# A decoder trunk on one Trainium2 core: PE's expert sum three groups behind its dots in place of two, U gathers six experts ahead of V gathers in place of four

## The chip, the cores and the metric

The kernel runs as one launch on one core of a Trainium2 chip. The metric is the device time of the launch in microseconds (us); lower is better. Everything is float32.

## What is computed

Two layers of a decoder trunk on 512 prompt tokens and 32 sample tokens (8 sequences of 4), model width 1024. Each layer is a modulated RMSNorm, one input projection that feeds a gated delta recurrence and a sliding-window attention, an output projection, and then a retrieval of experts, which is the part that the change touches:

```python
def _peer(h, wq, sub_keys, u_tab, v_tab):
...
    q = (xf @ wq).reshape(T, PK_HEADS, 2, PK_HALF).astype(f32)
    s = jnp.einsum('thpd,hpnd->thpn', q, sub_keys.astype(f32))
...
    eidx = jnp.take_along_axis(cidx, pos, axis=-1).reshape(T, PK_HEADS * PK_TOPK)
    gate = jax.nn.softmax(top_s, axis=-1).reshape(T, PK_HEADS * PK_TOPK)
...
    def block(args):
        xt, it, gt = args
        a = jnp.einsum('td,tkd->tk', xt.astype(f32), u_tab[it].astype(f32))
        a = jax.nn.gelu(a, approximate=False) * gt
        return jnp.einsum('tk,tkd->td', a, v_tab[it].astype(f32))
```

Every token picks 128 experts. For each of them a row of 1024 numbers is gathered from table U and dotted with the token's vector; the gelu of the dot times a gate is the weight with which a row gathered from table V is added to the token's sum.

## The kernel before, in words

**Units.** The tokens are worked through in ten units (`DUES`): per layer four tiles of 128 prompt tokens and one tile of the sample tokens. A unit's trunk (everything but the expert stage) is cut by names that all engines share, the seams: `norm1`, `conv0` to `conv2`, `hswq`, `hz`, `hmisc` for the head of the next unit, then `swq`, `z`, `misc`, `qkv`, `qk`, `decay`, `kk`, `half0`/`level0` to `half6`/`level6`, `ks`, `rhs`, `state`, `scores`, `softmax`, `pv`, `wo`, `norm2`, `wq0` to `wq3`, `keys`. The head of unit u+1 is interleaved with the end of the top-k of unit u (`tail`, on DVE: `pairs`, `halves`).

**Rounds.** The experts of a unit are worked in groups of G = 2. A prompt unit has 64 groups, a sample unit 16, 544 in all. Group i belongs to an earlier unit than the trunk that runs beside it. `due(u)` (line 93) deals the groups out over the seams: each engine's program calls its own `step(i)` at the same seam, 54 steps to a trunk unit of layer one, 48 to the first of layer two and 64 to the others. Nothing but semaphores ties the engines; the order on each is fixed by the program.

**One step.** DVE (line 1124): multiplies the gelu of group i-1 with its gates (`gated`, line 1088, row L1092), then dots group i (row L1133, two of them). ACT (line 728): makes the diagonal matrices of group i-1 (`diagonals`, row L725, two of them), then waits for the dots of group i and applies the gelu (row L733). PE (line 1391): adds group i-LAG into the two accumulator banks `ACC` (`add`, line 1378, row L1387, four matmuls per expert, since a float32 matmul of 512 columns shows as two rows for each of the two banks; eight per group). Pool (lines 500 to 536): sends the U gathers, and behind each the V gather of an earlier expert (rows L526, L535), 512 KB each.

```python
            for e in range(len(ROUNDS) * G + AHEAD_U):
...
                        pool.wait_ge(dots, i + 1)
...
                if e >= AHEAD_U:
                    v = e - AHEAD_U
...
                    pool.wait_ge(v_acc, v + 1)
```

**Rings.** All buffers of a group have R = 4 places: `ubuf`, `vbuf`, the weights `a4` and the diagonals `diag`. So the U gather of group i waits for the dots of group i-4, the V gather of an expert for the sum of the expert eight before it, and ACT's diagonals of group d (line 723, `act.wait_ge(v_acc, (i + 1) * G)`; the semaphore starts at 8) for PE's sum of group d-4.

**The end of a unit's experts.** DVE's `finish` (line 1108, rows L1115 and L1118) reads `ACC` once PE has added the unit's last group, and lets PE start the next unit's sum (`acc_free`, line 1383). It stands behind the dots of step k == 2 of the next unit's groups. ACT's `store` (row L714) writes the result at k == 4, and Pool loads the next unit's `xp` and `g2p` into the same buffers at k == LOAD_AT = 10 (rows L520, L521), after that store has landed. In the sample unit of each layer the indices, gates and token vectors make a trip through DRAM (`bounce` on SP), for which Pool and DVE wait ahead of the first group of that unit.

Of the kernel before, what the change touches and what calls it, by code (L numbers as in the profile page):

```python
# [40 lines left out]
G = 2  # L41
R = 4
SLOTS_UV = R * G
AHEAD_U = 4
LOAD_AT = 10
DUES = L * UNITS
LAG = 2
PG = EXPERTS // G
SG = PG // 4
LG = TILES * PG + SG  # L50
# [54 lines left out]
def trunk(nc, ins, outs):  # L105
    with ExitStack() as ctx:
# [185 lines left out]
        def closing(step, final):  # L292

            for i in range(DUE[-1], len(ROUNDS)):
                step(i)
                if i - DUE[-1] in (3, 5, 7):
                    final((i - DUE[-1] - 3) // 2)

        def place(u):
            return *divmod(u, UNITS), u % UNITS == TILES  # L300
# [165 lines left out]
        def _(pool):  # L466
# [32 lines left out]

            for e in range(len(ROUNDS) * G + AHEAD_U):  # L500
                if e < len(ROUNDS) * G:
# [4 lines left out]
                    if e % G == 0:  # L506
# [8 lines left out]
                        if k == LOAD_AT:  # L515
# [11 lines left out]
                                         in_offset=off).then_inc(u_in[e % SLOTS_UV], 16)  # L527
                if e >= AHEAD_U:
                    v = e - AHEAD_U
                    u, k = ROUNDS[v // G]  # L530
# [9 lines left out]
        def _(act):  # L540
# [167 lines left out]
            def store(u):  # L708

                layer, tile, batch = place(u)  # L710
                waiter(act, u)("x_out", 1)
                act.sem_inc(settled, 1)
                dst = outs["y"][tile] if u >= DUES - 2 else outs["xbuf"][layer + 1, tile]
                act.dma_start(dst, xp[:]).then_inc(s["x_stored"], 16)  # L714

            def final(n):
                act.wait_ge(fin_sq, n + 1)
                A.activation(ss, ss, ACT.Sqrt).then_inc(fin_root, 1)

            def diagonals(i):  # L720
                pick = sel if place(ROUNDS[i][0])[2] else ident
                act.wait_ge(ag_sb, i + 1)
                act.wait_ge(v_acc, (i + 1) * G)
                for j in range(G):
                    last = A.activation(diag[:, i % R, j, :], pick[:], ACT.Copy, scale=a4[:, i % R, 2, j:j + 1])  # L725
                last.then_inc(diag_sb, 1)

            def step(i):
                u, k = ROUNDS[i]
                if i:  # L730
                    diagonals(i - 1)
                act.wait_ge(dots, i + 1 + R)
                A.activation(a4[:, i % R, 1, :], a4[:, i % R, 0, :], ACT.Gelu).then_inc(gelu_sb, 1)  # L733
                if k == 2 and u == DUES - 1:
                    final(TILES - 1)
                if k == 4 and u:
                    store(u - 1)

            def modulation(l):
# [30 lines left out]
            act.wait_ge(const_in, 32)  # L770
            act.wait_ge(sel_in, 16)
            program(head, body, tail, step, modulation)
            closing(step, final)
            diagonals(len(ROUNDS) - 1)
            final(TILES)
# [4 lines left out]
        def _(dve):  # L780
# [307 lines left out]
            def gated(i):  # L1088

                u, k = ROUNDS[i]  # L1090
                dve.wait_ge(gelu_sb, i + 1)
                V.tensor_tensor(a4[:, i % R, 2, :], a4[:, i % R, 1, :], gates[:, u % 2, G * k:G * k + G],  # L1092
                                ALU.mult).then_inc(ag_sb, 1)
# [14 lines left out]
            def finish(u):  # L1108

                wait = waiter(dve, u)  # L1110
                groups = sum(1 for owner, k in ROUNDS if owner <= u)
                dve.wait_ge(v_acc, SLOTS_UV + G * groups)
                wait("xp_in", 32)
                for i in range(2):
                    last = V.tensor_tensor(g2p[:, 512 * i:512 * i + 512], ACC[i][:], g2p[:, 512 * i:512 * i + 512], ALU.mult)  # L1115
                last.then_inc(acc_free, 1)
                dve.wait_ge(acc_free, u + 1)
                last = V.tensor_tensor(xp[:], xp[:], g2p[:], ALU.add)  # L1118
                if u >= DUES - 2:
                    link(last)  # L1120
                    last = rms(TILES - 1 + u - (DUES - 2), xp[:])
                last.then_inc(s["x_out"], 1)

            def step(i):
                u, k = ROUNDS[i]
                if k == 0 and place(u)[2]:
                    dve.wait_ge(bounce_in, 16 * 12 * (u // UNITS + 1))
                if i:
                    gated(i - 1)
                for j in range(G):  # L1130
                    dve.wait_ge(u_in[i % R * G + j], (i // R + 1) * 16)
                    row = ubuf[:, i % R, j, :]
                    last = V.tensor_tensor_reduce(row, row, h2s[u], 1.0, 0.0, ALU.mult, ALU.add, a4[:, i % R, 0, j:j + 1])  # L1133
                last.then_inc(dots, 1)
                if k == 2 and u:
                    finish(u - 1)

            dve.wait_ge(const_in, 32)
            program(head, body, tail, step, modulation)
            closing(step, final)  # L1140
            gated(len(ROUNDS) - 1)
            finish(DUES - 1)
# [3 lines left out]
        def _(pe):  # L1146
# [231 lines left out]
            def add(i):  # L1378
                u, k = ROUNDS[i]
                end = SG if place(u)[2] else PG  # L1380
                pe.wait_ge(diag_sb, i + 1)
                if k == 0 and u:
                    pe.wait_ge(acc_free, u)
                for j in range(G):
                    pe.wait_ge(v_in[i % R * G + j], (i // R + 1) * 16)
                    for c in range(2):
                        last = T.matmul(ACC[c][:], diag[:, i % R, j, :], vbuf[:, i % R, j, 512 * c:512 * c + 512],  # L1387
                                        start=k + j == 0, stop=k == end - 1 and j == G - 1, skip_group_check=True)
                    last.then_inc(v_acc, 1)

            def step(i):
                if i >= LAG:
                    add(i - LAG)

# [3 lines left out]
            closing(step, lambda n: None)  # L1398
            for i in range(len(ROUNDS) - LAG, len(ROUNDS)):
                add(i)  # L1400
# [117 lines left out]
```

## Time and profile before

| | us |
|---|---|
| median of 3 runs | 4345.22 |
| lowest, highest | 4344.15, 4350.73 |
| the profiled execution, its own time | 4338.44 |
| its span, first to last instruction | 4336.6 |
| busy: PE | 3660.1 (84%) |
| busy: DVE | 2698.8 (62%) |
| busy: POOL | 2348.3 (54%) |
| busy: ACT | 1034.7 (24%) |
| mean granted TensorE clock | 0.932 of full |
| DMA, mean over the span | 352 GB/s |

Busy is the time in which an engine executed; register, branch and semaphore instructions are not in it. PE's clock is given as the share of full speed that was granted in a stretch. In a row of the timeline, the number in brackets is how long the engine had been idle just before, and behind the arrow stands what ended that idle time. A matmul row with x8 is one group of two experts.

### The profile page before, as it was taken

The page shows a single profiled execution, that of the slowest core. Times are in us where ns is not written, and L with a number is a line of the kernel's source. Part 1 is how long each engine was busy: PE and PEld are TensorE (multiplying, and loading weights), DVE is VectorE, ACT ScalarE, POOL GpSimd, SP SyncE. Part 2 cuts the span into 40 slices and gives each one's busy share as a digit, 9 for nine tenths or more (in the row PEclk, how much of TensorE's full clock was granted, in tenths as well). Part 3 has the DMA queues.
Part 4 walks back from the last instruction along what each step waited for, and adds up shares of the span by engine and source line. Part 5 has one row for each costly group of instructions (what it writes and reads, how often), then busy time and mean ns, then how long its engine had stood idle before and what let it go on. Part 6 is the DMA issues. An engine that isn't in the chain of part 4 may idle for free.

```text
span 4336.6 us, 45555 instructions
## 1 busy us (share of the span) xinstructions
PE 3660.1 (84%) x15180; PEld 2168.1 (50%) x15180; DVE 2698.8 (62%) x6307; ACT 1034.7 (24%) x2478; POOL 2348.3 (54%) x2218
## 2 busy tenths in 40 slices
PE   7778789888888888879888888888888888899766
PEld 1546356544644555656456444644564455456522
DVE  1234674876776586538667666776587657664575
ACT  0111322232132222112321322132213121312122
POOL 0000475477467547434764577467647764674455
PEclk9888899999999999889999999999999998998989
DMA  7626799999999999699999999999999999997988
GB/s 272 256 100 224 285 389 406 376 375 399 395 363 384 379 382 347 250 322 377 378 356 384 348 394 391 414 375 405 393 414 381 387 389 366 377 364 298 331 327 341
DMA packets 362538, 1527.72 MB, mean 352 GB/s; under 512 B 44952, under 2 KB 46872, under 8 KB 340512
## 3 DMA queue, kind: packets, MB, share of 16 engines
q0 software_dynamic: 316480, 1151.48, 69.7%
q1 hardware_dynamic: 39632, 316.42, 18.6%
q10 hardware_dynamic: 6192, 56.91, 3.5%
q8 instruction: 121, 1.98, 0.2%
q14 instruction: 113, 0.93, 0.1%
HBM read 1505.45 MB, written 21.22 MB: 352 GB/s over the span
## 4 chain that ended last, share of the span: by engine, by line
PE 48%; DVE 21%; DMA 14%; issue 7%; POOL 6%; ACT 4%; SPq 0%; DVEq 0%; POOLq 0%; ACTq 0%
PE ACC L1387 20%; DVE ubuf L1133 6%; PE B L1191 6%; DMA vbuf<-in_peer_v,idxs 5%; PE B L1367 4%; DMA ubuf<-in_peer_u,idxs 4%; PE ACC L1159 3%; DMA W<-in_w_big 3%; PE B L1354 3%; POOL ubuf L526 3%; POOL vbuf L535 3%; PE B L1198 2%; PE B L1222 1%; PE B L1169 1%; DVE qkvT L854 1%
## 5 line engine op out<-in xcount | busy, mean ns | idle before, releaser
L1387 PE MATMUL ACC<-vbuf,diag 128*128 128x512 f32 x4352 | 2092.6, 629 | 381.4 <-ACT diag L725 221.2
L526 POOL DMA_INDIRECT ubuf<-in_peer_u,idxs x1088 | 1181.8, 1086 | 1396.8 <-issue 735.1
L1387 PEld LDWEIGHTS ACC<-vbuf,diag 128*128 128x128 f32 x4352 | 838.6, 202 | 1431.4 <-issue 1017.1
L535 POOL DMA_INDIRECT vbuf<-in_peer_v,idxs x1088 | 1150.2, 1057 | 566.0 <-issue 325.8
L1133 DVE CUSTOM_DVE_ANT_0 ubuf<-ubuf,h2p 128x1024 f32<-128x1024 f32 x960 | 1141.8, 1221 | 183.1 <-DMA ubuf<-in_peer_u,idxs 182.6
L725 ACT ACTIVATE diag<-ident,a 128x128 f32<-128x128 f32 x1024 | 355.4, 395 | 966.2 <-DVE a L1092 959.7
L733 ACT ACTIVATE a<-a 128x2 f32<-128x2 f32 x544 | 110.5, 203 | 864.8 <-DVE a L1133 864.3
L1367 PEld LDWEIGHTS B<-hT,W 128*128 128x128 f32 x2560 | 296.4, 195 | 31.3 <-issue 29.6
L1191 PEld LDWEIGHTS B<-hT,W 128*128 128x128 f32 x2560 | 297.3, 196 | 25.9 <-issue 14.9
L1367 PE MATMUL B<-hT,W 128*128 128x128 f32 x2560 | 297.9, 278 | 10.7 <-DMA W<-in_w_big 10.1
L1191 PE MATMUL B<-hT,W 128*128 128x128 f32 x2560 | 298.5, 279 | 9.6 <-DMA W<-in_w_big 8.3
L922 DVE TENSOR_TENSOR uT<-uT,B 128x512 f32<-128x512 f32 x70 | 48.2, 688 | 258.8 <-PE B L1262 258.8
L1092 DVE TENSOR_TENSOR a<-a,gates 128x2 f32<-128x2 f32 x544 | 86.4, 159 | 186.4 <-ACT a L733 182.7
L1133 DVE CUSTOM_DVE_ANT_0 ubuf<-ubuf,hz 128x1024 f32<-128x1024 f32 x128 | 152.8, 1221 | 43.9 <-DMA ubuf<-in_peer_u,idxs 43.7
L1354 PE MATMUL B<-W,hT 128*128 128x512 f32 x320 | 140.0, 596 | 7.3 <-ACT hT L692 7.3
L1012 DVE MAX8 v<-J 128x8 f32<-128x128 f32 x160 | 34.9, 280 | 174.6 <-ACT J L706 173.8
L1159 PE MATMUL ACC<-ubuf,small 128*9 128x512 f32 x256 | 114.1, 603 | 14.4 <-DMA ubuf<-in_w_ada 14.4
L1261 PE MATMUL B<-U,uT 128*128 128x128 f32 x560 | 115.9, 291 | 10.3 <-ACT U L657 10.3
L733 ACT ACT_TABLE_LOAD x92 | 118.0, 1283 | 1.7
L1261 PEld LDWEIGHTS B<-U,uT 128*128 128x128 f32 x560 | 94.9, 203 | 40.1 <-issue 26.7
L1262 PE MATMUL B<-uT,U 128*128 128x128 f32 x560 | 113.9, 287 | 0.0
L1256 PEld LDWEIGHTS B<-uT,BT 128*128 128x128 f32 x560 | 74.3, 196 | 60.4 <-issue 37.1
(252 smaller groups left out, 3331.4 us busy)
## 6 DMA issues: line engine op xcount, KB each, us to landing
W<-in_w_big SPq DMA_DIRECT2D x110, 2048.0 KB, 10.8
ubuf<-in_w_ada ACTq DMA_DIRECT2D x16, 2048.0 KB, 8.4
ubuf<-in_peer_u,idxs POOLq DMA_INDIRECT x1088, 6.9
vbuf<-in_peer_v,idxs POOLq DMA_INDIRECT x1088, 7.0
vbuf<-in_w_ada ACTq DMA_DIRECT2D x8, 2048.0 KB, 8.7
W<-dram_mod SPq DMA_DIRECT2D x10, 1536.0 KB
W<-in_w_misc SPq DMA_DIRECT2D x10, 1056.0 KB, 8.2
W<-dram_mod SPq DMA_DIRECT2D x10, 1024.0 KB
```

What stands on the lines that cost most here:

```text
L526: g.indirect_dma_start(out=ubuf[:, i % R, e % G, :], out_offset=None, in_=ins["peer_u"], in_offset=off).then_inc(u_in[e % SLOTS_UV], 16)
L535: g.indirect_dma_start(out=vbuf[:, v // G % R, v % G, :], out_offset=None, in_=ins["peer_v"], in_offset=off).then_inc(v_in[v % SLOTS_UV], 16)
L725: last = A.activation(diag[:, i % R, j, :], pick[:], ACT.Copy, scale=a4[:, i % R, 2, j:j + 1])
L733: A.activation(a4[:, i % R, 1, :], a4[:, i % R, 0, :], ACT.Gelu).then_inc(gelu_sb, 1)
L1133: last = V.tensor_tensor_reduce(row, row, h2s[u], 1.0, 0.0, ALU.mult, ALU.add, a4[:, i % R, 0, j:j + 1])
L1159: last = T.matmul(ACC[n % 2][0:9, :], cT3[:, k, :], w[:, k, :], start=(k == 0), stop=(k == KC - 1))
L1191: last = T.matmul(B[2 + i][:, P * j:P * j + P], blocks(c)[:, j, k, :], hT[:, k, :], start=(k == 0), stop=(k == KC - 1))
L1261: T.matmul(B[2][:, P * hh:P * hh + P], XT[:, hh, :], U1[:, hh, :], start=True, stop=True)
L1262: last = T.matmul(B[3][:, P * hh:P * hh + P], U1[:, hh, :], XT[:, hh, :], start=True, stop=True)
L1354: last = T.matmul(B[i][:], hT[:, k, :], cols(f"wo{i}")[:, k, :], start=(k == 0), stop=(k == KC - 1))
L1367: last = T.matmul(B[(4, 5, 0, 1)[i]][:, P * j:P * j + P], blocks(f"wq{i}")[:, j, k, :], hT[:, k, :], start=(k == 0), stop=(k == KC - 1))
L1387: last = T.matmul(ACC[c][:], diag[:, i % R, j, :], vbuf[:, i % R, j, 512 * c:512 * c + 512], start=k + j == 0, stop=k == end - 1 and j == ...
```

## The change

LAG goes from 2 to 3: at step i PE adds group i-3. AHEAD_U goes from 4 to 6: Pool sends the V gather of expert e-6 behind the U gather of expert e. `finish` and `store` move one step later with it (k == 3 and k == 5). The rings keep R = 4 places. ACT's two conditions and DVE's one are written with LAG.

```diff
-AHEAD_U = 4
+AHEAD_U = 6
 LOAD_AT = 10
 DUES = L * UNITS
-LAG = 2
+LAG = 3
...
                 A.activation(a4[:, i % R, 1, :], a4[:, i % R, 0, :], ACT.Gelu).then_inc(gelu_sb, 1)
-                if k == 2 and u == DUES - 1:
+                if k == LAG and u == DUES - 1:
                     final(TILES - 1)
-                if k == 4 and u:
+                if k == LAG + 2 and u:
                     store(u - 1)
...
                 last.then_inc(dots, 1)
-                if k == 2 and u:
+                if k == LAG and u:
                     finish(u - 1)
```

PE, from the seam `norm1` of the head of unit 3 (the transposes of `h`, L1169) to the first matmul of `conv0` (L1191). `v_in0` and `v_in1` are the V rows of the two experts of a group in the ring's first place, `v_in2` and `v_in3` of the second, and so on; `diag_sb` is ACT's diagonals of the group. Before:

```order
L1169 MATMUL B<-ident,h 128x128 [waits h_normed]
L1169 MATMUL B<-ident,h 128x128 x7
L1387 MATMUL ACC<-vbuf,diag 128x512 [waits v_in0,diag_sb]
L1387 MATMUL ACC<-vbuf,diag 128x512
L1387 MATMUL ACC<-vbuf,diag 128x512 [waits v_in1]
L1387 MATMUL ACC<-vbuf,diag 128x512
L1387 MATMUL ACC<-vbuf,diag 128x512 [waits v_in2,diag_sb]
L1387 MATMUL ACC<-vbuf,diag 128x512
L1387 MATMUL ACC<-vbuf,diag 128x512 [waits v_in3]
L1387 MATMUL ACC<-vbuf,diag 128x512
L1191 MATMUL B<-hT,W 128x128 [waits keys_sb,in_conv0,hT_sb]
```

The same place in the changed kernel:

```order
L1169 MATMUL B<-ident,h 128x128 [waits h_normed]
L1169 MATMUL B<-ident,h 128x128 x7
L1387 MATMUL ACC<-vbuf,diag 128x512 [waits v_in6,diag_sb]
L1387 MATMUL ACC<-vbuf,diag 128x512
L1387 MATMUL ACC<-vbuf,diag 128x512 [waits v_in7]
L1387 MATMUL ACC<-vbuf,diag 128x512
L1387 MATMUL ACC<-vbuf,diag 128x512 [waits v_in0,diag_sb]
L1387 MATMUL ACC<-vbuf,diag 128x512
L1387 MATMUL ACC<-vbuf,diag 128x512 [waits v_in1]
L1387 MATMUL ACC<-vbuf,diag 128x512
L1191 MATMUL B<-hT,W 128x128 [waits keys_sb,in_conv0,hT_sb]
```

The same two sums stand between the transposes and `conv0`, each of the group one before.

DVE, at the seam `conv1` of the head of unit 6, beside which the experts of layer one's sample unit begin, before (from the second dot of k == 2 on):

```order
L1133 ISA ubuf,a<-ubuf,h2p 128x1024
L1133 ISA a 128x1
L1115 TENSOR_TENSOR g2p<-ACC,g2p 128x512 x2
L1118 TENSOR_TENSOR xp<-xp,g2p 128x1024
L1012 MAX v<-J 128x8 x4
```

and in the changed kernel, the end of `halves` at seam `conv2` and the step behind it:

```order
L1021 MAX v<-J 128x8 x4
L1025 MAX_INDEX i<-v,J 128x8 x4
L1092 TENSOR_TENSOR a<-a,gates 128x2
L1133 ISA ubuf,a<-ubuf,h2p 128x1024
L1133 ISA a 128x1
L1133 ISA ubuf,a<-ubuf,h2p 128x1024
L1133 ISA a 128x1
L1115 TENSOR_TENSOR g2p<-ACC,g2p 128x512 x2
L1118 TENSOR_TENSOR xp<-xp,g2p 128x1024
```

`finish` has moved behind the whole of `halves` and one more step. Pool's queue, the beginning of the gathers (removed and added rows):

```order
-L526 DMA ubuf<-in_peer_u,idxs 128x1024 x5
-L535 DMA vbuf<-in_peer_v,idxs 128x1024
-L526 DMA ubuf<-in_peer_u,idxs 128x1024
-L535 DMA vbuf<-in_peer_v,idxs 128x1024
-L526 DMA ubuf<-in_peer_u,idxs 128x1024
+L526 DMA ubuf<-in_peer_u,idxs 128x1024 x7
 L535 DMA vbuf<-in_peer_v,idxs 128x1024
```

The first V gather goes out behind seven U gathers in place of five, and at the end seven V gathers stand behind the last U gather in place of five.

## Rows read from the trace of the kernel before

**Rows 1.** The page, the chain that ended last by engine.
```profile
PE 48%; DVE 21%; DMA 14%; issue 7%; POOL 6%; ACT 4%; SPq 0%; DVEq 0%; POOLq 0%; ACTq 0%
```

**Rows 2.** The waits (engine line <- waited for: us in total, times, longest).
```profile
PE ACC L1387 <- ACT diag L725: 221.2, 47, 26.2
```

**Rows 3.** Timeline of PE, 1130 to 1260 us (start us, us, what, idle before).
```profile
1139.22 1.97 PE L1169 MATMUL B<-ident,h 128*128 128x128 f32 x8 [6.05 <-DVE h L827]
1140.98 4.32 PE L1387 MATMUL ACC<-vbuf,diag 128*128 128x512 f32 x8
1150.34 6.53 PE L1387 MATMUL ACC<-vbuf,diag 128*128 128x512 f32 x8 [5.05 <-ACT diag L725]
1156.71 7.31 PE L1191 MATMUL B<-hT,W 128*128 128x128 f32 x64
...
1246.04 13.34 PE L1387 MATMUL ACC<-vbuf,diag 128*128 128x512 f32 x24 [6.85 <-ACT diag L725]
```

**Rows 4.** Timeline of ACT, the diagonals before that stall.
```profile
1131.91 0.69 ACT L725 ACTIVATE diag<-ident,a 128x128 f32<-128x128 f32 x2 [5.88 <-DVE a L1092]
```

**Rows 5.** Timeline of DVE, from the end of the head on.
```profile
1212.25 0.16 DVE L1092 TENSOR_TENSOR a<-a,gates 128x2 f32<-128x2 f32 x1 [5.99 <-ACT a L733]
1224.01 0.29 DVE L1083 TENSOR_REDUCE small<-gates 128x8 f32<-128x128 f32 x1 [8.24 <-ACT gates L606]
...
1261.44 1.23 DVE L880 TENSOR_TENSOR J<-qkv 128x1024 f32<-128x1024 f32 x1 [0.99 <-ACT qkv L635]
```

**Rows 6.** Timeline of PE, the same stall in the heads of the other units.
```profile
779.54 5.40 PE L1387 MATMUL ACC<-vbuf,diag 128*128 128x512 f32 x8 [3.79 <-ACT diag L725]
...
1532.19 6.75 PE L1387 MATMUL ACC<-vbuf,diag 128*128 128x512 f32 x8 [4.57 <-ACT diag L725]
...
1997.06 3.70 PE L1387 MATMUL ACC<-vbuf,diag 128*128 128x512 f32 x8 [3.28 <-ACT diag L725]
...
2355.93 3.70 PE L1387 MATMUL ACC<-vbuf,diag 128*128 128x512 f32 x8 [3.52 <-ACT diag L725]
...
2386.52 6.24 PE L1387 MATMUL ACC<-vbuf,diag 128*128 128x512 f32 x8 [9.16 <-issue]
...
2778.19 6.68 PE L1387 MATMUL ACC<-vbuf,diag 128*128 128x512 f32 x8 [4.72 <-ACT diag L725]
...
3196.98 5.40 PE L1387 MATMUL ACC<-vbuf,diag 128*128 128x512 f32 x8 [4.55 <-ACT diag L725]
...
3628.39 6.54 PE L1387 MATMUL ACC<-vbuf,diag 128*128 128x512 f32 x8 [4.86 <-ACT diag L725]
```

**Rows 7.** Stretches: from:to length, PE, PEld, DVE, ACT, POOL busy, clock, DMA share, GB/s.
```profile
1150.00:1160.00 10.00, 9.66 (x38) 6.01 (x39) 9.11 (x28) 2.67 (x6) 5.04 (x5) 0.70 0.66 220
1250.00:1260.00 10.00, 10.00 (x28) 4.66 (x27) 9.37 (x26) 2.15 (x8) 7.87 (x8) 0.92 0.95 331
2770.00:2780.00 10.00, 5.28 (x10) 2.13 (x9) 9.23 (x24) 2.19 (x5) 0.00 (x0) 0.84 1.02 418
```

**Rows 8.** Timeline of ACT at seam wo of a layer-two unit.
```profile
2677.57 0.69 ACT L725 ACTIVATE diag<-ident,a 128x128 f32<-128x128 f32 x2 [0.23 <-DVE a L1092]
```

**Rows 9.** Timeline of PE, the sums of seam wo behind the output projection.
```profile
2685.72 10.46 PE L1387 MATMUL ACC<-vbuf,diag 128*128 128x512 f32 x24
```

**Rows 10.** Timeline of DVE, the residual add there and the norm's use of the root.
```profile
2688.37 1.29 DVE L997 TENSOR_TENSOR h<-B,W 128x512 f32<-128x512 f32 x2 [6.28 <-DMA W<-dram_mod]
...
2692.64 0.16 DVE L823 RECIPROCAL small<-small 128x1 f32<-128x1 f32 x1 [0.27 <-ACT small L557]
```

**Rows 11.** Timeline of ACT, the store of xp with the least room.
```profile
3790.11 0.33 ACTq L714 DMA_DIRECT2D dram_xbuf<-xp  x1
```

**Rows 12.** Timeline of POOL, the load into xp behind it.
```profile
3801.92 0.58 POOL L520 DMA_DIRECT2D xp<-dram_xbuf  x1
```

**Rows 13.** Timeline of PE, after the last trip through DRAM.
```profile
4215.88 14.93 PE L1387 MATMUL ACC<-vbuf,diag 128*128 128x512 f32 x28 [8.31 <-ACT diag L725]
```

**Rows 14.** Timeline of POOL, the last gather.
```profile
4311.05 0.94 POOL L535 DMA_INDIRECT vbuf<-in_peer_v,idxs  x1 [0.30 <-issue]
```

## The prediction

> **What bounds the kernel now.** I read the chain that ended last first: PE has 48% of it, DVE 21%, DMA 14%, POOL 6% [rows 1]. So no engine bounds alone; the question for each stretch is who waits for whom. Then the waits: PE sat idle 221.2 us for ACT's diagonals, 47 times [rows 2]. The diagonals are what LAG = 3 would have ready a step earlier, so 221.2 us is the pool of idle time that the change can touch, and most of the work is to find how much of it lies on the path.
>
> The timeline of PE shows one such stall in the head of every unit. In rows 3, PE transposes `h`, adds one group, and waits 5.05 us for the diagonals of the next; that group then takes 6.53 us in place of the 3.70 us that eight matmuls take where the clock is full [rows 3, 6], and `conv0` starts at 1156.71. The granted clock of that stretch is 0.70 [rows 7], a mix of the 1.2 and 2.4 GHz levels behind two idle pieces of 6.05 and 5.05 us. From 1156.71 to the end of the head PE has no idle time in the timeline, and DVE waits for what PE's projections release: 5.99 us for a gelu behind ACT's copy of `z`, then 8.24 us for ACT's exp behind the copy of `misc` [rows 5]. So from this stall to 1224 the path is PE's, with 14.2 us of room on DVE.
>
> Behind the head it is not. DVE's short convolution bounds from 1224 on, and Pool then sends a gather every 1.25 us without a pause (7.87 of 10 us busy, the rest its own issue gaps [rows 7]) until the output projection.
>
> **The change, part by part.**
>
> *The stall in the head.* PE's sums at that seam become those of one group before. The diagonals of the first of the two groups now standing there are older still, those of the second were made at 1131.91 [rows 4], before PE arrived at 1139.22 [rows 3]. The wait goes, and with it most of the slow clock. I cost each place as its idle time plus what the group behind it took over 3.70 us. That is 3.79 + 1.70 = 5.5 (unit at 779), 5.05 + 2.83 = 7.9 (1150), 4.57 + 3.05 = 7.6 (1532), 3.28 (1997, clock full) in layer one [rows 3, 6]: 24.3 us. All are below the 14.2 us that DVE has to give, so what comes next is unchanged and only starts earlier.
>
> At the unit of 2355.93 the idle 3.52 us goes too, but 9.16 us at 2386.52 belong to DVE's `finish`, which frees `ACC` [rows 6]. `finish` now stands behind `halves` and one more step, so PE meets it one seam later and waits about as long. I take 3 us; bounds 0 and 3.52 + 9.16 + 2.54 = 15.2.
>
> In layer two the three places give 4.72 + 2.98, 4.55 + 1.70 and 4.86 + 2.84, together 21.7 us [rows 6]. But while PE idles in the first of them, the DMA engines are at 1.02 with 418 GB/s and Pool sends nothing [rows 7]: they work off a queue, and it would be as long after the change. In layer one the same stretch has DMA at 0.66 [rows 7]. I take half, 11 us, with 0 and 21.7 as the ends.
>
> *Behind the convolution.* PE waits 6.85 us and then has three groups to add, 13.34 us, ahead of the transposes [rows 3]. Now it has two, 4.4 us less. DVE waited only 0.99 us for those transposes [rows 5], so 1 us is gained here, in the three units of layer one that show that row: 3 us. Bounds 0 and nine units by 4.4 = 40.
>
> *The other idle time of rows 2* is in stretches where DVE itself is late (top-k, attention scores, the closing groups): I cost it at nothing, its cover being DVE. Were that cover gone it would be worth up to the 221.2 less the 39 idle us counted above.
>
> *Pool's order.* V of a group goes out behind U of the group three later, in place of two, and PE needs it one step later. Group i-3's V still waits for a sum that PE does at step i-4, so neither ring holds more or less in flight: cost 0 in the stream. Where Pool stands still for the trip through DRAM, six V gathers are left behind it in place of four. After the last one Pool never pauses until its last gather at 4311.05 [rows 13, 14], so two more gathers of 1.25 us end up in that stretch: 2.5 us lost. At the start the first V gather is two U gathers later, hidden by diagonals that come later yet (the longest wait of rows 2 is 26.2 us).
>
> *The store of `xp`* moves one group later, some 5 us at Pool's pace, against Pool's load at LOAD_AT. The closest pair is 3790.11 and 3801.92, 11.8 us apart [rows 11, 12]; with the store late by 5, 6.8 us remain for a landing of about as much. I cost it at 0 and keep 2 us for the range.
>
> *The new wait.* The diagonals of group d go where those of d-4 lay, and PE now adds d-4 one step later. I compared, for all 540 groups, ACT's start with the end of the sum in that position. In four it would wait, all at seam `wo` of layer two: ACT is at its diagonals at 2677.57 [rows 8], while PE, busy with the output projection, ends the first of its three sums of that seam at 2685.72 + 10.46/3 = 2689.2 [rows 9]: 11.6 us. Behind it on ACT stand a gelu and the root of the norm. DVE starts the residual add at 2688.37, held by a load of `W`, and uses the root at 2692.64 [rows 10]. ACT would be done 0.69 us of diagonals and, as my estimate, 1.6 us of gelu, table load and root after 2689.2: about 2691.5. Cost 0, covered by a margin of 1 us.
>
> The sum: 24.3 + 3 + 11 + 3 - 2.5 = 38.8 us. The profiled execution took 4338.44 us and would take 4299.6. The median stands 6.8 us above it, and I forecast it as 4345.2 - 38.8 = 4306 us.
>
> **A rule against it.** In rows 7 the DMA engines moved 418 GB/s for 10 us. By the Trainium skill (DMA: Bandwidth & Descriptors, "Where 436 GB/s comes from") the HBM side limits a core to about 358 GB/s, and since this kernel moves 352 over its span, nothing would be left to gain. The trace disagrees with the figure (418 measured), not with the thought, which is the first rival.
>
> **The rivals.** Measurement of this kernel can tell about 0.2%, 8.7 us, from no change.
>
> 1. *DMA swallows it.* The idle time returns as waits for V rows or weights. For it: share 1.02 at 2770. Against: share 0.66 at 1150, and hardly any wait for weights. Only the empty DMA time at the four stalls of layer one is then gained, 3.4 us each, 13.6 - 2.5 = 11 us: 4334. Chance 0.17, half of it inside 0.2%.
> 2. *The lag reaches no path.* DVE's top-k and Pool's pace set the heads as well, PE merely arrives early. Against: the 14.2 us of DVE's waits. Then 4345 less 3 plus 2.5: 4345. Chance 0.09.
> 3. *More than counted.* PE's one group of lead also pays behind the convolution (40) and in the head at 2386 (15), and layer two gives all: about 75 us, 4270. Chance 0.12.
> 4. *The ring becomes the bound (slower).* PE three steps behind with four places leaves ACT one step. If ACT's late release at `wo` passes into the norm, 4 x 11.6 = 46 us are lost against 24.3 + 3 gained in layer one: 4345.2 + 46 - 28 = 4363. It decides from the point where DVE's norm no longer waits for `W`. For it: rows 8 and 9. Against: rows 10. Chance 0.06.
>
> The forecast has 0.56. Range: 4272 to 4336, which leaves out rivals 2 and 4 and the far ends. Faster by over 0.2%: 0.56 + 0.12 + half of 0.17 = 0.77; within: 0.17; slower: 0.06.
>
> **What would show it.** Right: in the heads of layer one no wait of PE for L725 between the transposes of `h` and `conv0`, DVE's waits at L1083 and L1092 shorter by what PE gained, PE's total wait for L725 well below 221.2 us, waits of ACT for L1387 of some 45 us at `wo`, and DVE's L821 to L823 there no later. Wrong: PE's waits for V rows up by as much as those for diagonals went down (rival 1); L1083 still 8 us late (rival 2); DVE waiting for the root behind L725 at `wo` (rival 4).

## The result, and the profile after

The change makes the kernel faster, by half of what was forecast: 4325.85 us (median of 17 runs, 4314.64 to 4337.45) against 4346.92 us for the kernel before on the same chip (17 runs, 4329.4 to 4353.29). The ratio is 0.9956, 95% interval 0.9946 to 0.9966, so 19 to 21 us. The forecast was 4306, with 38.8 us gained. Measured a second time, in another sitting (below), the ratio is 0.9964, 14 to 16 us. Single runs of one kernel lie up to 18 us from their median, so comparisons below go by ratios or by medians of one sitting, and single stalls by the traces.

The profiled execution took 4331.07 us, its span is 4329.3. The chain by engine, and the group of PE's sums, on the page of the changed kernel:

```profile
PE 49%; DVE 20%; DMA 15%; issue 7%; POOL 5%; ACT 4%; SPq 0%; DVEq 0%; POOLq 0%; ACTq 0%
...
L1387 PE MATMUL ACC<-vbuf,diag 128*128 128x512 f32 x4352 | 2066.1, 621 | 309.5 <-DMA vbuf<-in_peer_v,idxs 180.3
```

The waits of the changed kernel (us in total, times, longest):

```profile
PE ACC L1387 <- DMA vbuf<-in_peer_v,idxs: 180.3, 171, 12.3
...
PE ACC L1387 <- ACT diag L725: 84.0, 19, 26.2
...
ACT diag L725 <- PE ACC L1387: 69.6, 18, 14.2
...
PE B L1169 <- ACT small L676: 64.6, 10, 9.1
...
PE ACC L1387 <- issue: 40.1, 8, 10.6
```

PE's wait for diagonals fell from 221.2 to 84.0 us [rows 2]. Its wait for V rows rose from 123.5 to 180.3, and its wait for ACT's exp of the attention scores (L676) from 15.6 to 64.6. The waits behind "issue" are those for `finish` to free `ACC`. Most of the rise for V rows (from 53.7 to 105.4 us) lies between L1083 and `half0`, where the wait for diagonals fell from 117.8 to 51.0 us and the length of the stretch hardly changed (table below): there one wait took the place of another.

The head of unit 3, PE in the changed kernel, and the end of that head on DVE:

```profile
1139.46 1.97 PE L1169 MATMUL B<-ident,h 128*128 128x128 f32 x8 [6.06 <-DVE h L827]
1141.22 7.88 PE L1387 MATMUL ACC<-vbuf,diag 128*128 128x512 f32 x16
1148.94 7.31 PE L1191 MATMUL B<-hT,W 128*128 128x128 f32 x64
```

```profile
1208.09 0.16 DVE L1092 TENSOR_TENSOR a<-a,gates 128x2 f32<-128x2 f32 x1 [1.55 <-ACT a L733]
1216.24 0.28 DVE L1083 TENSOR_REDUCE small<-gates 128x8 f32<-128x128 f32 x1 [4.64 <-ACT gates L606]
```

The stall of [rows 3] is gone. `conv0` starts 7.77 us earlier than before, and so does L1083: the whole gain passes through the head, as DVE's two waits of [rows 5] fell by 4.4 and 3.6 us.

**Where it went.** I took the same six places in each unit of the traces, except the first unit, beside which no experts are worked: `conv0` (first L1191), the end of the head (L1083), `half0` (first L1256), `scores` (L974), `pv` (L989), `wq` (first L1367). The table has how much longer (+) or shorter (-) each stretch became, added over these nine units. The first two columns are two profiled executions of the changed kernel against the one before; those to the right belong to experiments below.

| stretch | after | after, again | finish early | finish early + filler | half V rows |
|---|---|---|---|---|---|
| `wq` to `conv0` | -55.9 | -55.1 | -44.5 | -53.9 | -57.2 |
| head, sample units | +17.7 | +21.7 | +18.5 | +21.5 | -0.6 |
| head, prompt units | -1.0 | +0.6 | -11.0 | -8.8 | +0.4 |
| L1083 to `half0` | -3.8 | -5.5 | +4.9 | +0.8 | +0.3 |
| `half0` to `scores` | +18.3 | +14.4 | -2.8 | -0.5 | +10.8 |
| `scores` to `pv` | +14.5 | +15.7 | +13.7 | -3.5 | +10.7 |
| `pv` to `wq` | -1.8 | -6.9 | -3.6 | +3.8 | -5.8 |

So the stretch up to `conv0`, which holds the priced stalls, gave 56 us, more than forecast, and some 50 were given back at three places that the forecast had priced at nothing: the heads of the two sample units, `half0` to `scores`, and `scores` to `pv`. The first two columns differ by up to 5 us in a stretch; two executions of the kernel with the early `finish` differ by 10 us in one (`half0` to `scores`: +7.3 in the first, -2.8 in the second, which the table shows). A single figure of the table is not to be trusted further than that. The first column adds up to -12 us only, less than the medians give: the profiled execution of the kernel before was 8 us below its kernel's median, that of the changed one 5 us above. The last column is the second pair with half V rows, the changed kernel against its sibling.

### The profile page after: what moved, and what is told of

Its sections match the earlier page's. It is cut to its first block, busy times and chain, and to the rows that moved or that the text cites. A ratio compares the mean times of both kernels' runs of the same rounds, so it can differ in the third digit from the quotient of the medians.

```text
span 4329.3 us, 45555 instructions
## 1 busy us (share of the span) xinstructions
PE 3657.7 (84%) x15180; PEld 2176.1 (50%) x15180; DVE 2698.7 (62%) x6307; ACT 1035.2 (24%) x2478; POOL 2364.5 (55%) x2218
## 3 DMA queue, kind: packets, MB, share of 16 engines
q0 software_dynamic: 316480, 1151.48, 69.6%
## 4 chain that ended last, share of the span: by engine, by line
PE 49%; DVE 20%; DMA 15%; issue 7%; POOL 5%; ACT 4%; SPq 0%; DVEq 0%; POOLq 0%; ACTq 0%
PE ACC L1387 20%; DVE ubuf L1133 7%; DMA vbuf<-in_peer_v,idxs 7%; PE B L1191 6%; PE B L1367 5%; PE ACC L1159 3%; DMA ubuf<-in_peer_u,idxs 3%; POOL ubuf L526 3%; POOL vbuf L535 2%; PE B L1354 2%; DMA W<-dram_mod 2%; DMA W<-in_w_big 2%; PE B L1169 2%; PE B L1198 2%; PE B L1222 1%
## 5 line engine op out<-in xcount | busy, mean ns | idle before, releaser
L1387 PE MATMUL ACC<-vbuf,diag 128*128 128x512 f32 x4352 | 2066.1, 621 | 309.5 <-DMA vbuf<-in_peer_v,idxs 180.3
L1387 PEld LDWEIGHTS ACC<-vbuf,diag 128*128 128x128 f32 x4352 | 825.7, 199 | 1349.6 <-issue 1043.7
L535 POOL DMA_INDIRECT vbuf<-in_peer_v,idxs x1088 | 1162.3, 1068 | 587.5 <-issue 337.3
L1191 PEld LDWEIGHTS B<-hT,W 128*128 128x128 f32 x2560 | 301.4, 198 | 31.8 <-DMA W<-in_w_big 15.3
L1191 PE MATMUL B<-hT,W 128*128 128x128 f32 x2560 | 302.7, 281 | 15.2 <-DMA W<-in_w_big 13.9
L1367 PEld LDWEIGHTS B<-hT,W 128*128 128x128 f32 x2560 | 294.4, 193 | 20.8 <-issue 18.9
L1367 PE MATMUL B<-hT,W 128*128 128x128 f32 x2560 | 295.3, 277 | 1.6 <-DMA W<-in_w_big 0.9
L1159 PE MATMUL ACC<-ubuf,small 128*9 128x512 f32 x256 | 114.1, 602 | 14.2 <-DMA ubuf<-in_w_ada 14.2
L997 DVE TENSOR_TENSOR h<-B,W 128x512 f32<-128x512 f32 x20 | 12.9, 686 | 148.8 <-DMA W<-dram_mod 134.5
```

The costliest lines, as they stand in the source:

```text
L535: g.indirect_dma_start(out=vbuf[:, v // G % R, v % G, :], out_offset=None, in_=ins["peer_v"], in_offset=off).then_inc(v_in[v % SLOTS_UV], 16)
L1159: last = T.matmul(ACC[n % 2][0:9, :], cT3[:, k, :], w[:, k, :], start=(k == 0), stop=(k == KC - 1))
L1191: last = T.matmul(B[2 + i][:, P * j:P * j + P], blocks(c)[:, j, k, :], hT[:, k, :], start=(k == 0), stop=(k == KC - 1))
L1367: last = T.matmul(B[(4, 5, 0, 1)[i]][:, P * j:P * j + P], blocks(f"wq{i}")[:, j, k, :], hT[:, k, :], start=(k == 0), stop=(k == KC - 1))
```

## The experiments

### The two edits apart

```diff
-AHEAD_U = 6
+AHEAD_U = 4
```

(first kernel: LAG = 3 alone), and in the second LAG = 2 with AHEAD_U = 6, `finish` and `store` as before.

> LAG = 3 alone, Pool's order as before (V gathers four experts behind U). Theory that Pool's order is the cost (V rows come about 5 us later than before relative to U rows, which is as much as PE's sum moved): PE's wait for V rows falls from 180.3 to below 125 us and the time is 8 us or more below the changed kernel. Theory that the lag alone makes both the gain and what is given back: within 5 us of the changed kernel. Theory that V sent early takes Pool's and DMA's time from U: U rows come later, DVE waits for them, and the time is 5 us or more above the changed kernel.

> Pool's order alone (V gathers six experts behind U), LAG = 2, finish and store one step earlier as before. All theories: PE keeps its waits for diagonals in the heads (some 221 us in all). If the order is neutral by itself, within 5 us of the kernel before. If it helps (U rows earlier), 5 us or more below. If V rows are what it delays, PE's wait for V rows rises above 180 us and the time is 5 to 20 us above the kernel before.

LAG = 3 alone is **slower** than the kernel before: 4367.17 us against 4343.61, ratio 1.005 (1.0033 to 1.0068). AHEAD_U = 6 alone is slower still: 4408.72, ratio 1.0154 (1.0131 to 1.0178), 65 us where I had expected 20 at most. The waits of the first:

```profile
POOL vbuf L535 <- PE ACC L1387: 653.8, 182, 25.8
DVE ubuf L1133 <- DMA ubuf<-in_peer_u,idxs: 430.8, 248, 11.2
...
PE ACC L1387 <- DMA vbuf<-in_peer_v,idxs: 73.4, 77, 6.9
```

and of the second:

```profile
PE ACC L1387 <- DMA vbuf<-in_peer_v,idxs: 239.7, 223, 12.9
...
PE ACC L1387 <- ACT diag L725: 195.1, 43, 24.6
```

The theory that Pool's order is a cost of the change falls, in the other direction than I had put it. With LAG = 3 and V sent four experts behind, Pool stands 653.8 us (before: 240.2) ahead of V gathers whose place PE frees a step later, and the U gathers queue behind it on the same engine: DVE's wait for U rows goes from 226.2 to 430.8. (Pool's waits for PE ahead of U gathers fell from 258.4 to 77.4 us; both kinds together rose from 499 to 731.) With LAG = 2 and V six behind, the V rows come a step after PE wants them. V of group i-LAG must go out with U of group i; then either ring is asked for at the same step. The two numbers are one setting.

### A ring of five for the diagonals

```diff
-        diag = sb("diag", [P, R, G, P])
+        diag = sb("diag", [P, RD, G, P])
...
-                act.wait_ge(v_acc, (i + 1) * G)
+                act.wait_ge(v_acc, SLOTS_UV + (i + 1 - RD) * G)
```

with RD = 5, and `i % RD` where `diag` is written and read.

> The changed kernel with a ring of its own for ACT's diagonals, 5 places in place of 4 (the other rings keep 4), so that ACT has again the slack against PE's sums that it had before the change. Ring theory (the gain that was given back between the scores and the output projection comes from ACT's diagonals held by PE, 69.6 us of waits in place of 6.2): ACT's waits for L1387 fall to below 15 us, PE's wait for ACT's exp of the scores (L1169 <- L676, 64.6 us) falls back to some 20 us, and the time is 12 to 20 us below the changed kernel. Stream theory (the gain is given back because Pool's gathers and the DMA engines set the pace of the groups): ACT's waits fall as well, but the time is within 5 us of the changed kernel and PE's wait for V rows (180.3 us) stays.

4329.27 us, ratio 0.9963 (0.9949 to 0.9978), where the changed kernel has 0.9956: the same. The waits (its lines stand one lower, since RD takes a line):

```profile
PE B L1170 <- ACT small L677: 61.9, 10, 9.1
...
ACT diag L726 <- PE ACC L1388: 13.9, 12, 5.9
```

The ring theory falls: ACT's waits for PE went from 69.6 to 13.9 us, and neither the time nor PE's wait for the exp followed. The new wait that the change adds costs nothing.

### `finish` a step earlier

```diff
-                if k == LAG and u == DUES - 1:
+                if k == 2 and u == DUES - 1:
...
-                if k == LAG + 2 and u:
+                if k == 4 and u:
...
-                if k == LAG and u:
+                if k == 2 and u:
```

> The changed kernel with finish at step k == 2 and store at k == 4 as before, PE's last sum of a unit still in its step k == 2. Theory that the store and the load of xp one step later cost time (Pool waits 5.6 us for the store, the level seams lose 7 us in the first unit): 5 us or more below the changed kernel. Theory that the place of finish is neutral: within 5 us. Theory that DVE then waits in finish for a sum that is only just being made: DVE's wait at L1115 rises by 2 us or more a unit, 10 to 20 us above the changed kernel.

4306.84 us, ratio 0.9911 (0.9894 to 0.9928). Measured again beside the changed kernel:

> The changed kernel itself, measured again beside the two that follow, so that the three can be compared on one chip in one sitting. Expected: 4326 us, 18 to 21 us below the kernel before.

> LAG = 3 with finish at k == 2 and store at k == 4, again. The trace of its first run had PE waiting 2.7 + 1.4 us for the accumulator to be freed, where the changed kernel had 40.1 + 4.4 us and the one before 24.1 + 12.2. If these waits are the difference: 4307 us, 15 to 20 us below the changed kernel. If the first measurement was a lucky chip: within 5 us of it.

The changed kernel 4330.11, ratio 0.9964 (0.9951 to 0.9977); with the early `finish` 4313.0, ratio 0.9917 (0.9898 to 0.9936). So 17 to 20 us lay in this placement (17 between the medians of one sitting, 20 by the ratios). The changed kernel itself came out 14 us below the kernel before in this sitting, not the 18 to 21 I had expected. In the changed kernel PE stands for `ACC` at the start of most units' sums; the timeline of PE has it eight times, among them

```profile
929.44 6.29 PE L1387 MATMUL ACC<-vbuf,diag 128*128 128x512 f32 x8 [5.73 <-issue]
...
2388.68 8.85 PE L1387 MATMUL ACC<-vbuf,diag 128*128 128x512 f32 x16 [10.57 <-issue]
...
2492.80 16.91 PE L1387 MATMUL ACC<-vbuf,diag 128*128 128x512 f32 x32 [4.41 <-issue]
```

and with the early `finish` (second run) these waits are, in total,

```profile
PE ACC L1387 <- issue: 2.3, 1, 2.3
PE ACC L1387 <- DVE g2p L1115: 1.4, 1, 1.4
```

3.7 us in place of 44.5 (40.1 and 4.4 for L1115), and of 36.3 before the change. With LAG = 3 PE has added a unit's last group in its step k == 2 and starts the next unit's in k == 3, so `finish` in DVE's step 2 has a step of room that "k == LAG" throws away. DVE pays for it with waits for PE's last sum (29.6 and 32.8 us in `finish`, 11.9 before this edit), which the third theory had foreseen, but its 10 to 20 us of loss did not follow. In the table the gain stands in the prompt heads (the stall at 2388) and between `half0` and `scores`. Of the other eight waits only three lie in that second stretch (5.73, 5.11 and 2.41 us, 13 in all; 6.5 before the change), so they explain a part of it. The edit also moves the store of `xp` a step earlier, and Pool's waits for that store (5.6 and 4.4 us in the two executions of the changed kernel) are gone with it; no run moves the one without the other.

### The clock behind the idle time that moved

PE at the seam `scores` of a unit of layer two. Before:

```profile
3466.72 3.70 PE L1387 MATMUL ACC<-vbuf,diag 128*128 128x512 f32 x8
3475.10 9.82 PE L1387 MATMUL ACC<-vbuf,diag 128*128 128x512 f32 x16 [4.68 <-ACT diag L725]
3485.68 1.97 PE L1169 MATMUL B<-ident,J 128*128 128x128 f32 x16 [0.76 <-ACT small L676]
```

After:

```profile
3459.36 3.70 PE L1387 MATMUL ACC<-vbuf,diag 128*128 128x512 f32 x8 [1.24 <-ACT diag L725]
3469.95 3.67 PE L1169 MATMUL B<-ident,J 128*128 128x128 f32 x16 [6.88 <-ACT small L676]
```

The granted clock right where the transposes run (from:to, length, PE, PEld, DVE, ACT, POOL busy, clock, DMA share, GB/s), before, after, and with the filler described below:

```profile
3485.00:3488.00 3.00, 2.32 (x18) 2.08 (x19) 2.30 (x2) 0.63 (x2) 2.33 (x3) 1.00 1.04 425
```

```profile
3470.00:3473.00 3.00, 3.00 (x15) 3.00 (x16) 2.90 (x5) 0.12 (x1) 2.38 (x3) 0.50 1.02 403
```

```profile
3444.00:3446.00 2.00, 1.69 (x15) 1.69 (x16) 1.71 (x1) 0.26 (x2) 1.39 (x3) 1.00 1.04 424
```

When the transposes can start is set by DVE and ACT: from the start of the scores' matmuls (3464.79 and 3449.06) it is 20.89 us in both. PE has no diagonals to wait for in between any more, so its idle time no longer lies ahead of sums that nobody waits for. It lies in one piece of 6.88 us ahead of the transposes, on the path, which then take 3.67 us in place of 1.97 at a granted clock of 0.50 in place of 1.00, the two levels of 1.2 and 2.4 GHz; the sums behind them begin slow too, and `pv` comes 1.4 to 2.9 us later after `scores` than before in seven of nine units. By the Trainium skill (TensorE: Matmul & The Clock Gate, "What's actually happening") an idle TensorE falls back to the lower level; the rows agree.

I tried to keep the old lag there: LAG = 2 from one seam to `wq3`, LAG = 3 from `keys` through the head, V gathers shifted with it, `finish` early.

```diff
+LAGS = [LAG] * len(ROUNDS)
+for trunk_unit in range(1, DUES):
+    seams = due(trunk_unit)
+    for step_at in range(seams["qk"].start, seams["keys"].start):
+        LAGS[step_at] = LAG - 1
```

> The lag by place: PE's sum three groups behind from the seam keys through the head to the seam qkv, two groups behind from qk to wq3; Pool's V gathers six and four experts behind with it (shifted by the four groups of the rings); finish at k == 2, store at k == 4. Clock theory (idle time of PE moved to just ahead of its transposes at qk and softmax makes these run at the low level, +14.5 us between scores and pv and about 1.5 us a unit at qk): the stretch scores to pv costs again what it did before, and the time is 8 to 20 us below the kernel with LAG = 3 and finish at k == 2 (4307). DMA theory (the rows' transfers set the time of the body): within 5 us of that kernel. Slower than it by 5 us or more: the lead of PE is used in the body too.

4316.27 us, ratio 0.9925 (0.9903 to 0.9947). `scores` to `pv` was back (-1.3 us over nine units), but L1083 to `half0` took 28.3 us more, since the group caught up at `qk` lies on the path (3.3 to 6.8 us more than in the changed kernel in six of nine units; a group's eight matmuls take 3.70), and the time is not below that of the kernel with the early `finish` (0.9911 and 0.9917). Hence the fall moved to the last step of `scores`:

> As the kernel with the lag by place, but the lag falls from three to two in the last of the three steps of the seam scores (in place of the seam qk) and rises again at keys; finish at k == 2. With the fall at qk the stretch from scores to pv went back to what it took before the change (14.5 us regained over nine units), but the group that is caught up cost 4 to 5 us a unit between the top-k and kk, 38 us in all. At scores PE stands idle 4.7 to 6.9 us ahead of its transposes, so the caught-up group should be free there. Clock theory: the stretch scores to pv as before the change, the stretch top-k to kk as with LAG = 3, and 10 to 16 us below the kernel with LAG = 3 and finish at k == 2. If what is regained there is lost again to the rows' transfers: within 5 us of it.

4318.24 us, ratio 0.9941 (0.9924 to 0.9958), no gain over the kernel with the early `finish`. The transposes ran at 1.96 us again, but the sums behind them now waited for V rows, four in a row of 0.3 to 0.7 us like

```profile
3458.05 1.96 PE L1397 MATMUL ACC<-vbuf,diag 128*128 128x512 f32 x4 [0.66 <-DMA vbuf<-in_peer_v,idxs]
```

and the stretch was 18.5 us longer than before the change, over nine units. The time is 5 us above the kernel with the early `finish` by the medians of one sitting and 10 to 13 by the ratios, so neither expectation held. The clock was won and handed to the gathers. The clock alone, with the order of the gathers untouched, is changed by a filler:

```diff
                 yield "scores"
+                for _ in range(6):
+                    T.matmul(B[4][:], ident[:], masks[:, 0:4 * P], start=True, stop=True)
                 wait("sc_exp", 1)
```

> LAG = 3 with finish at k == 2, and six matmuls of 512 columns more on PE (constants into a bank that nobody reads), at the end of the seam scores, where PE stands idle 6.9 us and then runs its transposes at the low clock (3.67 us in place of 1.97). Clock theory: the transposes are back at about 2 us, the stretch from scores to pv is back at 31.3 and 34.7 us (13.7 to 15.3 us less over nine units), and the time is 10 us or more below the kernel without them (4307 to 4313). Pace theory (the gathers that Pool sends without a pause, 1.33 to 1.37 us each from kk to pv, set the end of that stretch): the transposes are short again but the time is within 5 us of that kernel.

4300.93 us, ratio 0.9903 (0.9882 to 0.9924); the same seam (the sums stand at L1389, the filler at L1332):

```profile
3433.73 3.70 PE L1389 MATMUL ACC<-vbuf,diag 128*128 128x512 f32 x8 [0.51 <-ACT diag L725]
3437.27 5.31 PE L1332 MATMUL B<-masks,ident 128*128 128x512 f32 x12
3444.31 1.97 PE L1169 MATMUL B<-ident,J 128*128 128x128 f32 x16 [1.73 <-ACT small L676]
3446.12 10.46 PE L1389 MATMUL ACC<-vbuf,diag 128*128 128x512 f32 x24
```

The stretch from `scores` to `pv` is 17.2 us shorter than with the early `finish` alone (-3.5 against +13.7), so the clock is the cause of what was lost there. (In the first unit, which the table leaves out, the same stretch took 3.5 us more with the filler.) In the whole time the medians lie 6 and 12 us lower, but in different sittings; by the ratios, which allow for that, it is 3 and 6 us (0.9903 against 0.9911 and 0.9917), their intervals overlap, and the 10 us of the clock theory are not shown: shown in the place, not settled in the sum. By its median it is the fastest of the kernels that leave nothing out, 41 us below the kernel before.

### Half the V rows

What is left out is half of every V row: rows of 512 numbers are gathered, and PE multiplies them into both accumulator banks. Every engine has its work as before; the gathers move a quarter less. The relief for the DMA engines is smaller than that: on the page, the gathers' queue moves 866.27 MB in place of 1151.48, but its packets still take 59 to 60% of the engines' time in place of 69.7%.

```diff
-                    g.indirect_dma_start(out=vbuf[:, v // G % R, v % G, :], out_offset=None, in_=ins["peer_v"],
+                    g.indirect_dma_start(out=vbuf[:, v // G % R, v % G, 0:512], out_offset=None, in_=ins["peer_v"].rearrange("n (h d) -> (n h) d", h=2),
```

> The kernel before with V rows of 512 numbers in place of 1024 (256 KB a gather in place of 512; PE multiplies the same half row into both accumulator banks, so the engines do the same work; what is left out is half of every V row, a quarter of what the gathers move). It takes the load from the DMA engines, busy at a share of 0.94 to 1.02 in nearly every stage of both kernels. DMA theory (the gain of the change was given back as waits for rows): this kernel is faster than before by 100 us or more, and the change measured between this one and its sibling is 40 us or more. Engine theory (what is given back is idle time of PE and its slow clock at other seams, set by DVE and ACT): this one is faster by under 60 us, and the change between the two is again about 20 us.

> The changed kernel with the same half V rows. DMA theory: 40 to 55 us below the kernel before with half rows (what the heads gained, 55.9 us, now stays). Engine theory: 15 to 25 us below it.

4317.3 and 4278.15 us, ratios to the kernel before 0.9938 (0.9914 to 0.9962) and 0.9835 (0.9815 to 0.9855). Again, in more rounds:

> The kernel before with half V rows, again, in more rounds and in one sitting with its sibling, since the first pair rested on four runs each. Expected: some 4317 us as in the first measurement.

> The changed kernel with half V rows, again. The first pair gave 39 us between the medians, where the full rows give 19 to 21. Transfer theory (what the full rows lose is lost to late rows): again 35 us or more below its sibling. If the first pair was chance: 15 to 25 us below it.

4314.0 and 4275.86 us, ratios 0.9929 (0.9914 to 0.9943) and 0.9845 (0.9828 to 0.9862). So the change is worth 39.2 and 38.1 us where the rows are short, and 14 to 21 where they are whole. The gain is just under the 40 us of the first expectation. But short rows alone were to give 100 us, if transfers ruled; they gave 28 to 32. The DMA engines are not the bound of the whole. They are late in places, and the table says where: the heads of the two sample units. PE in the head of the layer-one sample unit, changed kernel:

```profile
1533.65 5.32 PE L1387 MATMUL ACC<-vbuf,diag 128*128 128x512 f32 x12
1543.71 3.78 PE L1387 MATMUL ACC<-vbuf,diag 128*128 128x512 f32 x4 [4.74 <-DMA vbuf<-in_peer_v,idxs]
1547.28 12.98 PE L1191 MATMUL B<-hT,W 128*128 128x128 f32 x107
```

(the window cuts the last row; all 128 matmuls take 15.33 us)

and with half rows (second run):

```profile
1528.91 7.03 PE L1387 MATMUL ACC<-vbuf,diag 128*128 128x512 f32 x16
1535.78 14.45 PE L1191 MATMUL B<-hT,W 128*128 128x128 f32 x128
```

That stretch of the kernel before, and of the changed one (from:to, length, PE, PEld, DVE, ACT, POOL busy, clock, DMA share, GB/s):

```profile
1538.00:1606.00 68.00, 68.00 (x368) 48.49 (x367) 49.97 (x149) 14.60 (x35) 34.07 (x34) 1.00 1.02 415
```

```profile
1526.00:1601.00 75.00, 70.26 (x367) 49.67 (x366) 53.91 (x159) 15.23 (x38) 36.87 (x36) 0.95 1.02 400
```

The engines of the DMA were already full there (share 1.02; with half rows 0.95 at 341 GB/s over the same head). PE arrives earlier, the row does not, and a sum that waits also costs the clock: 4.74 us of waiting, 1.9 more for the sum behind it and 0.9 more for the 128 matmuls (15.33 in place of 14.45) make 7.5 of the 7.6 us. The eight profiled executions with LAG = 3 in the head, V six behind and whole rows lost 7.6 to 11.9 us at this head. With half rows it was 0.0 in one, and 14.9 in the other, where PE waited 11.68 us for a load of `W`: there too a transfer. That execution took 4295.6 us, 16 to 20 more than the other three of its kernel, so late transfers can still come with half rows. The sample head of layer two lost 7.2 to 11.0 in those eight, and nothing (-0.5, -0.6) in the two with half rows.

## Why the prediction was wrong

The forecast gain of 38.8 us came as 14 to 21. There are two errors of opposite sign in it: the stalls were worth some 17 us more than priced, and some 50 us came back at places priced at nothing. They cancelled in part, and that is luck.

- **Direction and mechanism: right.** The stalls in the heads went, as did the slow clock behind them, and the gain reached the end of each head. Rival 2 is out.
- **The heads, 24.3 + 3 + 11: too small.** The trace has 55.9. The step that failed low is "I take half" in layer two, for DMA engines at 1.02 in a window of 10 us [rows 7]. Its three heads gave 6.2, 6.7 and 9.2 us, the whole of their price. Of layer one the priced 5.5, 7.9 and 7.6 came as 8.1, 8.1 and 8.8, the 3.28 at 1997 as 4.7, and the 3 at 2355.93 as 4.1. (The 8.8, ahead of the first sample head, was 5.2 in the second execution, and 0.8 and 0.0 with the early `finish`.)
- **"I cost it at nothing, its cover being DVE" is the step that failed.** The cover held, but I priced only PE's waiting. Idle time that stays on PE still changes place. In [rows 2] it lay ahead of sums; now it lies ahead of the transposes of the scores, and the stretch from `scores` to `pv` took 14.5 us more. Behind the convolution too: DVE's 0.99 us of [rows 5] went, as priced, but PE then stood 5.43 us ahead of the transposes of `qkv`, and these took 1.97 us in place of 1.09, with the two groups of matmuls behind them slow as well. In place of 1 us gained a unit, 1.5 us were lost from L1083 to `kk` in each of two units of layer one, of which 0.8 were left at `half0`. The table's -3.8 us from L1083 to `half0` looks like the 3 us of the forecast, but 5.7 of it come from the last unit, which was not priced: a match by chance.

```profile
1257.42 1.97 PE L1169 MATMUL B<-ident,qkv 128*128 128x128 f32 x8 [5.43 <-DVE qkv L886]
```

- **That "what comes next is unchanged and only starts earlier" failed in the sample units' heads, and rival 1 had named it.** It had DMA swallow the gain everywhere; it does so in these two heads, 17.7 to 21.7 us. That is about as much as the gain with half rows (38 to 39 us) exceeds the one with whole rows, but other stretches differ between the two by up to 8 us as well, so the sum does not prove the place. PE's waits for V rows rose by 57 us while those for diagonals fell by 137. I had looked at a share of 0.66 in ten microseconds of one head, and carried it to heads with another load. The engines of the DMA moved 415 GB/s over the 68 us above. The Trainium skill has this too: by its page HBM Reference, "Specifications (TRN2)", a core that streams alone gets well above the share of 358 GB/s that I had cited; the trace agrees.
- **`finish`: the wait was foreseen, its sum was not.** "PE meets it one seam later and waits about as long": 9.16 us became 10.57. I priced that one place. Over all units the waits rose from 36.3 to 44.5 us, and the early `finish`, which removes them, was worth 17 to 20 us.
- **Pool's order, 2.5 us: about right.** The last unit takes 4.3 us more from L1083 to the end in the trace (11.6 us ahead at the former, 7.3 at the last `finish`). From the last L1367 to the end the order alone cost 3.0 us and the lag alone 0.8. That this order is what makes LAG = 3 pay at all (1.005 without it) the forecast did not say.
- **The store of `xp`, 0 with 2 us kept:** Pool waited twice for the store, 5.6 us in all. What that cost was not measured by itself.
- **The ring, 0: right.** The waits at `wo` came as foreseen in number and place, four of 13.8 to 14.2 us where I had worked out 11.6 (ACT met fourteen shorter ones elsewhere, 13 us in all),

```profile
2681.72 0.69 ACT L725 ACTIVATE diag<-ident,a 128x128 f32<-128x128 f32 x2 [14.03 <-PE ACC L1387]
```

and DVE used the root as before, with 0.27 us of idle:

```profile
2685.52 0.17 DVE L823 RECIPROCAL small<-small 128x1 f32<-128x1 f32 x1 [0.27 <-ACT small L557]
```

Rival 4 is out, and the ring of five confirms it.

- **Two sums of the prediction do not add up.** The idle times counted there make 34.3 us, not 39; nothing hangs on it. Rival 3, with all that it names (24.3 + 15.2 + 21.7 + 40 - 2.5), comes to 98.7 us and 4247, not to 75 and 4270.

**What stays open.** `half0` to `scores` took 14 to 18 us more in the changed kernel, 8 and 11 with half rows, 6 with the ring of five, and +7.3 and -2.8 in the two executions with the early `finish`. The waits for `ACC` met there account for 7 us of it (13 in place of 6.5). Pool has no pause there in the unit whose stretch begins at 1292, and no fewer instructions: 71 in the 96 us from 1292 before, 71 in the 95 us from 1285 after, 1.35 and 1.34 us each, and they come no faster with half rows (71 in 95 us). But that unit lost nothing. The one that lost most (7.1 us, its `half0` at 2939 before and 2923 after) has 81 gathers in 106 us before and 82 in 113 after, with more waits of PE for V rows. That Pool's pace is the limit of this stretch is my reading; no run changed the pace, and the cause stays open.

## What to carry to other kernels

When a stall is removed from an engine whose work is paced by others, its idle time can move rather than go: look at what stands right behind the new idle piece. If that is on the path, the lower clock is paid there (3.67 us in place of 1.97 here), and useless work in the gap can be cheaper than the gap (17 us in that stretch, 3 to 6 in the whole). A lag, the prefetch distance that feeds it and the point where its accumulator is handed over are one setting: moved together they gave 0.9911 to 0.9917, the last left behind 0.9956 to 0.9964, the lag alone 1.005. And a DMA share must be read in each kind of stretch from which a gain is claimed: 0.66 in one head said nothing of another at 1.02.

## What the runs showed of the hardware

A quarter of the gathered bytes left out made the kernel only 28 to 32 us faster in 4345, though the DMA engines were busy for 90% or more in 31 of the page's 40 slices. With half rows only 8 slices are so full, and the time hardly follows: a share near one did not tell here that the whole time is set by the transfers. It did not tell the bytes either, since a quarter less of them took the gathers' share of the engines' time only from 69.7 to 59 or 60%. Pool's gathers came no faster. And a gather that Pool sends without a pause keeps it busy for 0.93 to 0.95 us in three cases of four, for 2.00 at times and for 3.0 at most:

```profile
1301.36 2.00 POOL L526 DMA_INDIRECT ubuf<-in_peer_u,idxs  x1 [0.30 <-issue]
1303.67 0.94 POOL L535 DMA_INDIRECT vbuf<-in_peer_v,idxs  x1 [0.30 <-issue]
```
